# Warm-up matmuls unrolled, the first k-tile's split shared by two engines, and the second part of x moved to ScalarE's queue

## What is computed

```python
h = rmsnorm(x, norm_mix_g[l])                       # x: (1, 256, 2048)
proj = jnp.einsum('bsd,de->bse', h, w_in[l])        # w_in: (2048, 8192)
dq, dk, dv, mq, mk, mv, gate = jnp.split(proj, SPLITS, axis=-1)
```

## Time and profile before

| | us |
|---|---|
| median of 3 runs | 570.93 (570.92 to 571.76) |
| the profiled execution | 571.09 |
| its span, first to last instruction | 569.3 |
| PE busy | 561.1 (99%) |
| PE weight loads busy | 468.1 (82%) |
| DVE busy | 427.7 (75%) |
| ACT busy | 409.4 (72%) |
| mean DMA rate | 217 GB/s |

### The profile page before, as it was taken

The page is one execution under the profiler, slowest core; times in us unless marked ns, Lnnn a source line. Parts: engine busy times, 40 slices in busy tenths (PEclk is TensorE's granted clock), DMA queues, the critical chain, the costliest instruction groups (busy, mean ns, idle before and its releaser), DMA issues.

```text
span 569.3 us, 8640 instructions
## 1 busy us (share of the span) xinstructions
PE 561.1 (99%) x2650; PEld 468.1 (82%) x2650; DVE 427.7 (75%) x720; ACT 409.4 (72%) x658; POOL 2.1 (0%) x26
## 2 busy tenths in 40 slices
PE   9999999999999999999999999999999999999995
PEld 7888888888888888888888888888888888888884
DVE  4769778688886876866766768667578886878975
ACT  5796865877868778775784784876598796856543
POOL 1000000000000000000000000000000000000000
PEclk9999999999999999999999999999999999999998
DMA  8997769678676776875875976779899986983903
GB/s 260 353 286 249 209 186 199 187 229 233 191 229 193 202 217 185 237 223 158 256 213 157 259 201 202 207 202 288 271 240 257 272 241 195 259 228 109 254 2 147
DMA packets 152292, 123.58 MB, mean 217 GB/s; under 512 B 67865, under 2 KB 134218, under 8 KB 151754
## 3 DMA queue, kind: packets, MB, share of 16 engines
q1 hardware_dynamic: 151946, 122.73, 76.6%
q10 hardware_dynamic: 320, 0.53, 0.3%
HBM read 105.93 MB, written 2.10 MB: 190 GB/s over the span
## 4 chain that ended last, share of the span: by engine, by line
PE 97%; DMA 1%; ACT 0%; SPq 0%; issue 0%; DVE 0%; ACTq 0%
PE ps L650 28%; PE ps L651 28%; PE ps L652 28%; PE ps L732 2%; PE ps L890 1%; PE ps L891 1%; PE ps L895 1%; PE ps L714 1%; PE ps L685 1%; PE ps L689 1%; PE ps L693 1%; DMA xs<-in_x 1%; PE ps L672 1%; PE ps L850 0%; PE ps L717 0%; PE ps L856 0%
## 5 line engine op out<-in xcount | busy, mean ns | idle before, releaser
L1260 DVE TENSOR_TENSOR w_lo<-w_raw,w_hi 128x1024 fp32r<-128x1024 f32 x183 | 222.7, 1223 | 102.1 <-ACT w_hi L920 99.8
L920 ACT ACTIVATE w_hi<-w_raw 128x1024 fp32r<-128x1024 f32 x183 | 192.3, 1057 | 77.8 <-PE ps L652 76.6
L650 PE MATMUL ps<-w_hi,aT 128*128 128x512 f32 x540 | 211.7, 392 | 0.0
L651 PE MATMUL ps<-w_lo,aT 128*128 128x512 f32 x540 | 210.3, 389 | 0.0
L652 PE MATMUL ps<-w_hi,aT 128*128 128x512 f32 x540 | 210.1, 389 | 0.0
L652 PEld LDWEIGHTS ps<-w_hi,aT 128*128 128x128 f32 x540 | 101.4, 188 | 21.2
L650 PEld LDWEIGHTS ps<-w_hi,aT 128*128 128x128 f32 x540 | 101.4, 188 | 20.9
L651 PEld LDWEIGHTS ps<-w_lo,aT 128*128 128x128 f32 x540 | 101.4, 188 | 20.5
L650 PE MATMUL ps<-w_hi,yT_hi 128*128 128x512 f32 x144 | 56.1, 390 | 0.0
L651 PE MATMUL ps<-w_lo,yT_hi 128*128 128x512 f32 x144 | 56.0, 389 | 0.0
L652 PE MATMUL ps<-w_hi,yT_lo 128*128 128x512 f32 x144 | 56.0, 389 | 0.0
(11 more groups left out here) (220 smaller groups left out, 580.8 us busy)
## 6 DMA issues: line engine op xcount, KB each, us to landing
w_raw<-in_w_in SPq DMA_DIRECT2D x251, 256.0 KB, 3.2
w_raw<-in_w_out SPq DMA_DIRECT2D x64, 256.0 KB, 4.0
w_raw<-in_w_kv_mem SPq DMA_DIRECT2D x32, 256.0 KB, 4.3
w_raw<-in_w_q_mem SPq DMA_DIRECT2D x16, 256.0 KB, 2.9
w_raw<-in_w_o_mem SPq DMA_DIRECT2D x16, 256.0 KB, 3.7
mems<-in_mem SPq DMA_DIRECT2D x1, 2048.0 KB, 10.9
xs<-in_x SPq DMA_DIRECT2D x3, 512.0 KB, 6.0
w_raw<-in_w_in SPq DMA_DIRECT2D x10, 128.0 KB, 4.8
```

The source lines that it names most:

```text
L650: pe.matmul(acc, hi[:, k0 + k, tok], w_hi[:, slot, k], start=first and k == 0, stop=False)
L651: pe.matmul(acc, hi[:, k0 + k, tok], w_lo[:, slot, k], start=False, stop=False)
L920: act.activation(w_hi[:, i % SPLITS], raw, ACT.Copy).then_inc(hi_made, 1)
L1260: dve.tensor_tensor(lo, w_raw[:, i % RAW], hi.bitcast(F32), ALU.subtract).then_inc(lo_made, 1)
```

## The change

There are three edits. The dummy matmuls, five before and two behind the transposes as a hardware loop, become three, two and two, written out one by one: three at the start, two between the gains' transposition and the rows' transposes, two behind those. The high part of the very first weight k-tile (512 columns) is no longer written by ACT alone: ACT does columns 0:256, DVE copies columns 256:512 as soon as the weights have landed, with a semaphore `k0_hi_dve` on which PE's first matmuls and DVE's own `w_lo` wait. The second part of x (columns 256:512) leaves SP's list; ACT waits until the first part has landed and issues it on its own queue.

```diff
-X_PART_BEFORE = (0, 1, 2, None, 3, None, None, 4)
+X_PART_BEFORE = (0, None, 2, None, 3, None, None, 4)
+X_PART_BY_ACT = 1
...
-WARM_UP = (5, 2)
+WARM_UP = (3, 2, 2)
...
             def keep_busy(count):
-                with pe.Fori(0, count):
+                for _ in range(count):
                     pe.matmul(ps[:, 2, 0:P], ones, ones, start=True, stop=True)
...
                     pe.wait_ge(k_hi if i == 0 and n < SINGLE else hi_made, n + 1)
+                    if k == 0:
+                        pe.wait_ge(k0_hi_dve, 1)
...
             pe.transpose(ps[:, 3, 0:KO], mix_gain[:, :], ident[0:KO, 0:KO]).then_inc(gainsT_made, 1)
+            keep_busy(WARM_UP[1])
             transpose_rows(0)
             transpose_rows(1)
-            keep_busy(WARM_UP[1])
+            keep_busy(WARM_UP[2])
...
-                    act.activation(w_hi[:, n % SPLITS, i], w_raw[:, n, i], ACT.Copy).then_inc((k_hi, hi_made)[i], 1)
+                    cols = slice(0, 2 * P) if n == 0 and i == 0 else slice(0, COLS)
+                    act.activation(w_hi[:, n % SPLITS, i, cols], w_raw[:, n, i, cols], ACT.Copy
+                                   ).then_inc((k_hi, hi_made)[i], 1)
...
+            a, b = X_PARTS[X_PART_BY_ACT]
+
+            act.wait_ge(x_loaded[0], 16)
+            act.dma_start(xs[:, :, a:b], x_tiles[:, :, a:b]).then_inc(x_loaded[X_PART_BY_ACT], 16)
             act.wait_ge(gainsT_ready, 1)
...
             def first_split_lo(n):
                 for i in range(GK // 2):
+                    if n == 0 and i == 0:
+                        dve.wait_ge(k_loaded[0], 16)
+                        dve.tensor_copy(w_hi[:, 0, 0, 2 * P:COLS], w_raw[:, 0, 0, 2 * P:COLS]).then_inc(k0_hi_dve, 1)
                     rows_out_lo(2 * n + i)
                     dve.wait_ge((k_hi, hi_made)[i], n + 1)
+                    if n == 0 and i == 0:
+                        dve.wait_ge(k0_hi_dve, 1)
```

More of the change, by code:

```diff
@@ L312, in program @@
         k_lo = sem("k_lo")
+        k0_hi_dve = sem("k0_hi_dve")
         hi_made = sem("hi_made")
```

## The result

The changed kernel took 575.24 us (median of 8 runs, 573.65 to 577.93), the kernel before 571.27 beside it (8 runs, 570.92 to 572.15): ratio 1.0069, interval 1.0057 to 1.0081, **4 us slower**. The forecast was 570.5, with a range up to 571.3.

What follows compares the result with a forecast made beforehand. PE, busy 99%, was taken as the bound, so only its opening counted: 0.65 us ahead at k-tile 2, less some 0.2 waiting for x's third part, left 0.45 off the 570.93 median: 570.5, range 569.9 to 571.3.

Steps and rivals of the forecast that it cites:

- the transit of the second part on ACT's queue: Time from ACT's issue of x's second part to its landing: taken as 3.3 us, landing at 6.7.
- D: Rival: x's second part meets the backlog, lands at 8.3, k-tile 2's transposes wait, all 0.65 us later: 571.6; chance 0.10.
- C: Rival: x's third part still lands at 10.7, the stall only moves there, total 570.9; chance 0.15.
- E: Rival: TensorE stays at 1.2 GHz through k-tiles 0 and 1, 572.9, or k-tile 0 alone, 571.5; chance 0.05.
- The clock's give-back: In k-tile 0, the first 0.35 us of real work run at half rate, giving back 0.17 us.
- the 0.65 us ahead: At k-tile 2's transposes, PE would start at 7.0 instead of 7.65, with no wait for x's second part.
- Hidden cost on ACT: ACT's wait and 0.43 us issue fit its idle time before its work at 4.42, 0.5 us to spare.
- Warm-up: In the opening, the regrouped, unrolled dummies start the first real matmul near 5.37, 0.35 us earlier.
- Split: First k-tile's copy, 0.41 us on ACT and 0.29 on DVE, hides behind the last dummies; worth under 0.1.
- What is late next: Before k-tile 4's transposes, PE waits some 0.2 us for x's third part, leaving about 0.45 us gained.

Runs made afterwards that it cites:

- e13: Changed kernel with SP issuing the second part of x once the first has landed, ahead of k-tile 3's weights: 571.46 us, ratio 1.0002.
- e4: Changed kernel with SP issuing the second part of x behind the weights of k-tiles 2 and 3: 573.49 us, ratio 1.0044.
- e1: Changed kernel with the second part of x back in SP's list, warm-up and split kept: 571.11 us, ratio 0.9998.
- e8: Changed kernel with the second part of x third in SP's list, ahead of k-tile 1's weights: 571.40 us, ratio 1.0002.
- e11: Kernel before with only the warm-up of 3, 2 and 2 written out: 571.44 us, ratio 1.0005.
- e9: Kernel before with SP issuing the second part of x third, ahead of k-tile 1's weights: 571.25 us, ratio 1.0003.
- e12: Kernel before with SP issuing x's second part third and its third part in two, the first ahead of half 2's weights: 571.28 us, ratio 0.9998.
- e10: Changed kernel with SP's third part of x moved behind half 2's weights: 573.26 us, ratio 1.0035.
- e2: Kernel before with only the move of the second part of x to ACT's queue: 574.22 us, ratio 1.0048.
- e5: The changed kernel, unaltered, measured again for its spread against the kernel before: 572.91 us, ratio 1.0045.
- e6: Changed kernel with SP holding all loads behind half 0 until the second part of x has landed: 574.76 us, ratio 1.0065.
- e14: The changed kernel, unaltered, run beside e13 on the same chip, against the kernel before: 574.74 us, ratio 1.0045.

## Why the prediction was wrong

**The step that failed** is the transit of the second part on ACT's queue. I took 3.3 us, between 2.6 and 4.9; measured were 7.0, 6.5 and 7.7 in three profiles of the changed kernel, and 6.5 with the move alone. The part was to land at 6.7 and landed at 10.91: 0.5 us of that is its later issue (3.89 and not 3.4, as the first part took 3.1), 3.7 the transit. Both of my bounds came from SP's own queue. A row for a transfer of that size on a second queue beside a full first one did not exist in the trace, and I closed the range at the longest transit that I had instead of leaving it open. On SP's own queue at about the same moment it takes 4.6 us ahead of k-tile 3's weights (e13) and 5.1 behind them (e4); what is beyond that goes with ACT's queue. How the DMA engines come to it stays open.

**The rival was there, with too small a price.** D named this place and this direction, and put the turn at a transit of 4.2 us. Its price, 0.65 us, rested on 4.9. With 7.0 its own rule gives 3.89 + 7.02 = 10.91, and 3.3 us. It had a chance of 0.10. The sentence of the Trainium skill that I set beside C (DMA: Bandwidth & Descriptors, Issuing engines are not separate DMA queues: they share the engines and interleave) was a warning that no bandwidth is won. The changed trace agrees: from 6 to 8 us the two queues together took 93.6% of the engines, as SP's alone did from 4 to 5.9 (93.4%). The cost beyond that it does not tell.

**The clock** I priced in E for the wrong cause. Without the late part the new warm-up loses nothing in the total (e1); the slow stretch behind the stall cost 1.4 us in the first profile, just what E had for one k-tile. D and E are one event there, and come to 4.7. In other executions only D's part is there.

**The clock's give-back** in k-tile 0 was mis-sized too, and the late part hid it. I had 0.17 us; in the changed profile k-tile 0 takes from 5.58 to 7.86 (7.40 and one pair of 0.46), 2.28 us where the earlier trace rows have 1.47, so 0.8. PE would have wanted the second part at 7.86, not at 7.0, which is later than its transposes started before (7.65). In e8, where the part was in time, they started at 8.00. So the 0.65 us ahead was not there to be had in either profile.

**Hidden cost on ACT:** right. ACT's wait and issue (3.89 to 4.30) ended before its first work at 4.70.

**Warm-up:** the first real matmul came at 5.58, not 5.37. The gains' transposition ran at 2.64 instead of 2.55 and the two dummies behind it took 1.22 us instead of the 1.06 of the earlier trace rows (from start to start 1.06, where I had 0.86), so the row transposes started at 3.91, not 3.63; in eight of twelve profiles PE also waits for the gains, which I had not named. Its worth was put at 0.35 less 0.17; on the time of the whole kernel it is nothing that can be measured (e1, e11).

**Split:** both durations were right (0.41 and 0.29 against 0.41 and 0.29), its place was not: I had it hidden, worth under 0.1, and it starts PE 0.26 us sooner. In the total that does not show.

**What is late next:** right in kind, and it is the step that carries furthest. With the second part in time PE waited for the third (e9), and with that in time for DVE's aT (e12). So had the transit been as I took it, the change would have been worth less than my 0.45: e9 and e8, which have the second part in time, measure no gain (1.0003 and 1.0002, each within 0.12% of no change). The forecast of "within 0.2%" would have held, the number would have been some 0.5 us too low.

## What to carry to other kernels

A transfer that an engine needs at a known time should stand in the queue that carries the rest, at the place where it is needed: issued on a second queue at 3.4 to 4.0 us, beside a full one, it took 5.9 to 7.7 us here in all six profiles, and its last packets set the landing. A late place in the same queue costs too (e4). Where the trace has no row for such a case, the longest transit seen is not an upper bound; leave the range open and give the open end a chance. Price a stall of TensorE twice, with a slow clock behind it and without, as here both came in executions of one kernel. And before valuing a stall that goes, look for the next operand that lands just in time: here there were three in a row.

## What the runs showed of the hardware that was not expected

Two queues on the same DMA engines did not share them evenly: with 256 KB issued on ACT's at 3.89 us, SP's moved all of 0.53 MB from 4 to 5.9 us, then ACT's got 0.23 MB of 0.54 from 6 to 8, then 0.03 of 0.83. A short spell of service, late at both ends. Without SP's stream the same transfer took 3.0 us.

SP's own issuing slowed while ACT's transfer was under way. The two issues of half 1's second k-tile took 0.94 us on SP at 3.24, the same two of half 2 took 2.16 at 5.22 in the changed kernel, where they took 1.07 in the kernel before (at 5.71). In the other profiles with ACT's issue at 3.4 to 3.8 and the third part of x in its old place they took 1.49 to 2.08, in e10, with the third part moved back, 0.94, and without ACT's transfer up to 1.32 (e11):

```profile
3.24 0.94 SPq L528 DMA_DIRECT2D w_raw<-in_w_in  x2
...
5.22 2.16 SPq L528 DMA_DIRECT2D w_raw<-in_w_in  x2
```

TensorE's clock after a wait was not set by the wait's length alone. Pairs of matmuls ran at half rate (0.85 us) behind 2.9 us of waiting in the change and behind 1.2 in e2, and at full rate (0.46) behind 1.4 in e5, 1.9 in e6 and 2.6 in e10. In e14, behind 2.5 us, the clock was full when PE went on at 11.57 and fell about 0.9 us later, to 0.50 until 15.7:

```profile
12.30:15.70 3.40, 3.40 (x10) 2.62 (x9) 1.66 (x3) 1.74 (x4) 0.00 (x0) 0.50 0.75 206
```

How the engines choose between the queues was not measured, and stays open. So does what decides in which executions of the change the clock falls.
